# Spreading the residual gates' rows by DMA, and turning the modulation rows by transposes, in a two-layer fp32 encoder trunk

## What is computed

```
mod = (silu(c) @ w_mod[l] + b_mod[l])
sh1, sc1, g1, sh2, sc2, g2 = split(mod, 6)
h  = rmsnorm(x, norm1_g[l]) * (1 + sc1) + sh1
mixed = three branches of h (attention, convolution, state space), gated and summed
x  = x + g1 * (mixed @ w_out[l])
h2 = rmsnorm(x, norm2_g[l]) * (1 + sc2) + sh2
x  = x + g2 * ((silu(gate(h2)) * up(h2)) @ w_ffn_out[l])
```

## Time and profile before

| what | value |
|---|---|
| median of three runs | 1031.75 us |
| the profiled execution: its time | 1028.69 us |
| its span, first to last instruction | 1026.9 us |
| mean granted TensorE clock | 0.972 of full speed |
| PE busy | 946.5 us, 92% |
| DVE, ACT busy | 669.1 us, 464.6 us |
| DMA share of 16 engines (SP's queue) | 55.8%, 192.85 MB |

### The profile page before, as it was taken

How to read it: one execution, slowest core, us unless ns; L and a number is a source line. 1 busy time by engine, 2 the same in 40 slices (tenths; PEclk the granted TensorE clock), 3 DMA queues, 4 the chain that set the end, 5 groups by cost and what they waited for, 6 DMA issues and landing times.

```text
span 1026.9 us, 16212 instructions
## 1 busy us (share of the span) xinstructions
PE 946.5 (92%) x6911; PEld 795.2 (77%) x6911; DVE 669.1 (65%) x910; ACT 464.6 (45%) x544; POOL 8.7 (1%) x11
## 2 busy tenths in 40 slices
PE   5688998999998899999998999999999799999995
PEld 2487985666776878898996997666676599999994
DVE  3783878999575485456446576899966654444445
ACT  4484135623643465545335332564264453434342
POOL 2000000000000000000000000000000000000000
PEclk9798899999999999999999999999999999999998
DMA  9955235548666446465657534454867625555521
GB/s 340 234 201 206 83 125 204 204 135 292 256 253 156 164 167 244 166 228 204 223 166 162 165 104 175 174 211 158 273 230 280 212 92 179 191 186 184 192 96 41
DMA packets 128023, 194.01 MB, mean 189 GB/s; under 512 B 30706, under 2 KB 90618, under 8 KB 121808
## 3 DMA queue, kind: packets, MB, share of 16 engines
q1 hardware_dynamic: 127608, 192.85, 55.8%
q10 hardware_dynamic: 344, 0.14, 0.1%
HBM read 191.93 MB, written 1.05 MB: 188 GB/s over the span
## 4 chain that ended last, share of the span: by engine, by line
PE 65%; DVE 23%; ACT 4%; DMA 3%; issue 3%; SPq 0%; ACTq 0%; DVEq 0%
PE bank L537 18%; PE bank L538 17%; PE bank L539 17%; DVE wlo L1316 7%; DVE yc L1597 7%; PE bank L573 3%; DMA raw<-in_w_mod 2%; PE bank L629 2%; PE bank L602 2%; ACT whi L978 1%; PE bank L652 1%; DMA raw<-in_w_out 1%; PE bank L640 1%; DVE h L1490 1%; PE bank L728 1%
## 5 line engine op out<-in xcount | busy, mean ns | idle before, releaser
L1316 DVE TENSOR_TENSOR wlo<-raw,whi 128x2048 fp32r<-128x2048 f32 x132 | 302.1, 2290 | 237.5 <-PE bank L539 191.1
L978 ACT ACTIVATE whi<-raw 128x2048 fp32r<-128x2048 f32 x132 | 252.3, 1911 | 160.0 <-DMA raw<-in_w_in 73.0
L537 PE MATMUL bank<-hhi,whi 128*128 128x256 f32 x992 | 287.5, 290 | 7.1 <-DVE hlo L1495 4.0
L538 PE MATMUL bank<-hlo,whi 128*128 128x256 f32 x992 | 282.8, 285 | 0.0
L539 PE MATMUL bank<-hhi,wlo 128*128 128x256 f32 x992 | 282.7, 285 | 0.0
L537 PEld LDWEIGHTS bank<-hhi,whi 128*128 128x128 f32 x992 | 192.4, 194 | 16.3 <-issue 10.4
L538 PEld LDWEIGHTS bank<-hlo,whi 128*128 128x128 f32 x992 | 192.6, 194 | 0.6
L539 PEld LDWEIGHTS bank<-hhi,wlo 128*128 128x128 f32 x992 | 192.4, 194 | 0.0
L537 PE MATMUL bank<-whi,bhi 128*128 128x512 f32 x304 | 121.4, 399 | 3.4 <-DVE wlo L1316 3.4
L538 PE MATMUL bank<-wlo,bhi 128*128 128x512 f32 x304 | 119.1, 392 | 0.0
L539 PE MATMUL bank<-whi,blo 128*128 128x512 f32 x304 | 118.8, 391 | 0.0
(11 more groups left out here) (247 smaller groups left out, 839.4 us busy)
## 6 DMA issues: line engine op xcount, KB each, us to landing
raw<-in_w_mod SPq DMA_DIRECT2D x48, 1024.0 KB, 7.3
raw<-in_w_ffn_in SPq DMA_DIRECT2D x44, 1024.0 KB, 5.2
raw<-in_w_in SPq DMA_DIRECT2D x38, 1024.0 KB, 5.4
raw<-in_w_ffn_out SPq DMA_DIRECT2D x22, 1024.0 KB, 5.0
raw<-in_w_out SPq DMA_DIRECT2D x8, 1024.0 KB, 6.9
raw<-in_w_in SPq DMA_DIRECT2D x16, 256.0 KB, 5.1
raw<-in_ssm_glu_b SPq DMA_DIRECT2D x4, 1024.0 KB, 5.1
raw<-in_ssm_glu_a SPq DMA_DIRECT2D x4, 1024.0 KB, 5.1
```

Source lines behind the costliest of these rows:

```text
L537: mm(o, w_hi, a_hi, start=start, stop=False, skip_group_check=True)
L538: mm(o, w_hi, a_lo, start=False, stop=False, skip_group_check=True)
L978: fn(whi[mi % N_HI][:, :], raw[SLOT[item]][:, :], ACT.Copy).then_inc(s_hi, 1)
L1316: V.tensor_tensor(wlo[mi % N_LO][:, :], raw[SLOT[("main", *divmod(mi, NB))]][:, :], whi[mi % N_HI][:, :].bitcast(F32), ALU.subtract).then_ ...
```

## The change

`g_rows` on PE, `g_copy` on ACT, the list `G_AT` and the semaphore `g_tr` go. In their place SP issues, for each gate, two DMAs that read one row of `modrow` (one partition, 2 KB) 128 times and write it to 128 partitions. The places are in SP's list: `g1` before piece k = 4 of group 2 of its layer; `g2` of layer 0 before piece k = 4 of layer 1's group 0; `g2` of layer 1 behind the load of block `fo 0` (block 37). The bias load moves from piece k = 4 to k = 6, and its wait on `g_tr` becomes a wait for the landing of the spread. `mod_columns` makes four 128x128 transposes, and `mod_vectors` reads every 32nd column of their result.

```diff
+        def spread_gate(eng, l, ng):
+            eng.wait_ge(mod_row, 3 * l + ng + 1)
+            eng.wait_ge(s_ready, 2 * l + 2)
+            eng.wait_ge(ys_lo, l + 1)
+            for half in range(2):
+                r = 32 * (2 * (ng - 1) + half)
+                dst = (g1 if ng == 1 else g2)[:, half * 512:(half + 1) * 512]
+                eng.dma_start(dst, modrow[r:r + 1, :].rearrange("p (o n) -> p o n", o=1).to_broadcast([1, P, 512])).then_inc(g_ready, 16)
...
                     _, l, ng, k = item
-                    if k == 4 and (l, ng) != (0, 0):
+                    if k == 4 and ng == 2:
+                        spread_gate(sp, l, 1)
+                    if k == 4 and l and ng == 0:
+                        spread_gate(sp, l - 1, 2)
+                    if k == 6 and (l, ng) != (0, 0):
                         sp.wait_ge(mod_tr, 3 * l + ng)
                         if ng != 1:
-                            sp.wait_ge(g_tr, 4 * l + (2 if ng == 2 else 0))
+                            sp.wait_ge(g_ready, 16 * (4 * l + (2 if ng == 2 else 0)))
                         load_bias(sp, l, ng)
...
+                    if item[1:] == (DEPTH - 1, AT[("fo", 0)]):
+                        spread_gate(sp, DEPTH - 1, 2)
                     if item[1:] == (DEPTH - 1, AT[("fg", 0)]):
                         sp.wait_ge(s_ready, 2 * DEPTH)
...
                 for j in range(4):
-                    last = mm(b_mod[:, 4 * j:4 * j + 4], modrow[:, j * P:(j + 1) * P], consts[:, 0:4], start=(j == 0), stop=(j == 3), skip_group_check=True)
+                    last = nc.tensor.transpose(b_mod[:, j * P:(j + 1) * P], modrow[:, j * P:(j + 1) * P], ident[:, :])
                 last.then_inc(mod_tr, 1)
-
-            def g_rows(l, ng, half):
-                pe.wait_ge(mod_row, 3 * l + ng + 1)
...
-                mm(b_y[:, :], ones[r:r + 1, :], modrow[r:r + 1, :], start=True, stop=True, skip_group_check=True).then_inc(g_tr, 1)
...
-            def g_copy(l, ng, half):
...
-                fn(dst[:, half * 512:(half + 1) * 512], b_y[:, :], ACT.Copy).then_inc(g_ready, 1)
...
-                V.tensor_copy(modv[:, c0:c0 + 16].rearrange("p (q j) -> p j q", q=4), b_mod[:, 0:16].rearrange("p (j q) -> p j q", q=4)).then_inc(mod_ready, 1)
+                V.tensor_copy(modv[:, c0:c0 + 16].rearrange("p (q j) -> p j q", q=4), b_mod[:, :].rearrange("p (j r) -> p j r", j=4)[:, :, 0:P:32]).then_inc(mod_ready, 1)
```

More of the change, by code:

```diff
@@ L160 @@
 MIX_TURN_AT = {2 * AT[("cp", 1)] + 1: (0, 1), 2 * AT[("wo", 0)]: (2,), 2 * AT[("wo", 0)] + 1: (3,)}
-G_AT = {2 * (i + 2 + half) + 1: (m[0], half) for i, m in MOD_AT[0].items() if m[1] == DK - 1 for half in range(2)}
 PREP_AT = AT[("fg", 1)]
@@ L371, in trunk @@
             sem(n) for n in "ldt_spread vec_tr vec_cp c_tr silu_c c_ready".split())
-        row_zero, s_bias, mod_row, mod_tr, mod_ready, scale_ready, g_tr, g_ready = (
-            sem(n) for n in "row_zero bias_landed mod_row mod_tr mod_ready scale_ready g_tr g_ready".split())
+        row_zero, s_bias, mod_row, mod_tr, mod_ready, scale_ready, g_ready = (
+            sem(n) for n in "row_zero bias_landed mod_row mod_tr mod_ready scale_ready g_ready".split())
         sq_ready, rb_ready, rms_ready, diag_ready, xt_ready, h_full, hhi_ready, hlo_ready = (
@@ L846, in small_columns @@
                 if l:
-                    pe.wait_ge(g_ready, 4 * l)
+                    pe.wait_ge(v_ready, l)
                 nc.tensor.transpose(b_y[:, 0:VROWS], rows, ident[0:VROWS, 0:VROWS])
@@ L892, in side @@
                     mix_turn(l, g)
-                if t in G_AT:
-                    g_rows(l, *G_AT[t])
                 if t in (CONV_MEAN_AT, CONV_VAR_AT):
@@ L1209, in side @@
                     mix_hi(l, g)
-                if t in G_AT:
-                    g_copy(l, *G_AT[t])
                 if l == 0 and t in ROUND_AT[0]:
@@ L1658, in post @@
                         if t == 0 and u == 0:
-                            dve.wait_ge(g_ready, 4 * l + 2)
+                            dve.wait_ge(g_ready, 16 * (4 * l + 2))
                         tt(flat(tmp), bank[BANK_OF[(l, i - 1, t)]][:, :], g1[:, cols], ALU.mult).then_inc(wo_read, 1)
@@ L1674, in post @@
                 elif kind == "fo" and n == NF - 1:
-                    dve.wait_ge(g_ready, 4 * l + 4)
+                    dve.wait_ge(g_ready, 16 * (4 * l + 4))
                     for t in range(TILES):
```

## The result

The changed kernel takes 1064.88 us (median of 4 runs, 1060.56 to 1066.43); the kernel before, beside it, 1031.76 us (1031.64 to 1034.16). The ratio is 1.0309, with a 95% interval from 1.0273 to 1.0344: slower. The profiled execution is 1066.0 us with a span of 1064.2 us, 37.3 us above the profiled execution of before (1028.69 and 1026.9). The mean granted clock is 0.948 of full speed against 0.972, and among the four executions the time follows it (1066.43 at 0.949, 1063.75 at 0.953, 1060.56 at 0.958).

What follows compares the result with a forecast made beforehand. PE was taken as the bound (65% of the chain, DVE 23%). Lateness of 28.8 + 8.6 minus 6.15 removed gave 31.3 us: 1060.0 profiled, 1063 us median with 3.1 added; own range 1050 to 1074, with the fast rival 1024 to 1072.

Steps and rivals of the forecast that it cites:

- R: Time to spread both halves of one gate from one source partition each: 18.6 us, 9.3 us a half; forecast's chance 0.60.
- the load over 64 partitions: Attention weights' load in the profile before: 226 GB/s against 396 over 128 partitions; divided by eight places, 28.3 GB/s each.
- The loads behind them: Loads after a spread in SP's queue wait for it: block 25's lands at 767.4 us, block 46's at 422.4.
- The rival of the full rate: Spreads run at nearly full rate, R up to 4: all loads in time, 6.15 us gained, 1025.6 us; chance 0.27.
- The bound below R: Lower bound from the store of 256 KB from 128 partitions: some 1.5 us engine time for two at 396 GB/s.
- Twice the room: Rival: reads have twice the room, R = 9.3; `g1` costs 2 x 5.1, sum +4.1, 1035.8 us; chance 0.08.
- `g1`: 14.4 us forecast: In each layer, block 25's load comes late behind the spread, PE begins block 26 14.4 us late; both layers 28.8 us.
- `g2` of layer 0: 8.6 us forecast: Block 46's load comes late behind the spread, so DVE's `lo` starts at 424.3 instead of 415.66: 8.6 us.
- `g2` of layer 1: nothing, as forecast: Behind block 37's load the spread ends at 834.8, block 38's load at 837.4, read at 845.64: hidden, no cost.
- What is removed: Work taken from PE and ACT: row products for `g2` 4.2 us, column sets 1.05 and 0.9; together 6.15 us gained.
- The first set: First set of column products on PE's chain, 1.85 us, halved by transposes: 0.9 us gained.
- the third: One of three column sets on PE's chain, 0.79 us by products against 0.44 by transposes: 0.35 us gained.

Runs made afterwards that it cites:

- the half-size spreads: The changed kernel with each spread moving 256 of its 512 numbers, in as many packets: 1034.77 us, ratio 1.0033 against the kernel before.
- the kernel without spreads: The changed kernel without any spread or the waits for it, gates holding other contents: 1025.7 us, ratio 0.9946 against the kernel before.
- neither part alone: The kernel before with only columns by transposes: 1032.74 us; with only row products, copies and their waits gone and the bias load moved: 1029.46 us.
- the kernel with 128 sources: The changed kernel with each spread reading 128 partitions of modrow one to one, same bytes: 1024.12 us, ratio 0.9936 against the kernel before.
- The transposes alone: The kernel before with only the columns made by transposes, row products kept: 1032.74 us, ratio 1.0015 against the kernel before.

## Why the prediction held, point by point

**The price of the spread.** The term that decides all was R, forecast as 18.6 us for a gate from the load over 64 partitions: 28.3 GB/s for one place in SBUF. The windows show 26 to 29 GB/s for some 14 us, and a mixed edge at either end; the two halves of a gate land 9.0 us apart, where 9.3 were forecast. The loads behind them land as forecast. In layer 1 the load of block 25 landed at 773.77 + 19.29 = 793.06; the forecast was 767.4 on the clock of before, and SP's issue ahead of the spread had moved from 738.49 to 765.03, by 26.5 us: 793.9. For block 46 it was 422.4, plus 12.2 us of lateness: 434.6; ACT took it up at 434.27. The rival of the full rate fell; what spoke for it, that the row was of writes, counts for nothing, as reads have the same limit. (The bound below R, "some 1.5 us" for two halves at 396 GB/s, should be 1.3; nothing rests on it.) Twice the room (R = 9.3) fell as well, and the half-size spreads show that its number would have been right had the rate been so: expected +4.1 us against before, measured 3.1.

**`g1`: 14.4 us forecast, 12.9 and 12.7 measured.** The path was as told. In layer 1 the load landed 0.8 us before its forecast, and PE began block 26 at 807.63, which is 807.63 - 767.45 - 26.5 = 13.7 us late; a further 0.9 us is made up by the next milestone.

**`g2` of layer 0: 8.6 us forecast, 11.4 measured.** This is the step that failed in size, "so DVE's `lo` of block 46 starts at 424.3 instead of 415.66". I took ACT's copy as the one thing that `lo` waits for. The timeline of the kernel after, ACT, DVE and PE:

```profile
431.69 1.91 ACT L980 ACTIVATE whi<-raw 128x2048 fp32r<-128x2048 f32 x1 [12.36 <-DMA raw<-in_w_ffn_in]
433.51 0.58 ACT L1030 ACTIVATE blx<-bank 128x512 f32<-128x512 f32 x1
434.27 1.91 ACT L980 ACTIVATE whi<-raw 128x2048 fp32r<-128x2048 f32 x1 [0.18 <-DMA raw<-in_w_ffn_out]
...
439.27 2.29 DVE L1308 TENSOR_TENSOR wlo<-raw,whi 128x2048 fp32r<-128x2048 f32 x1 [3.34 <-PE bank L553]
...
424.22 0.28 PE L553 MATMUL bank<-hhi,wlo 128*128 128x256 f32 x1
434.23 1.09 PE L754 MATMUL bank<-ident,ca 128*128 128x128 f32 x4 [9.73 <-ACT blx L1030]
434.97 0.56 PE L551 MATMUL bank<-hhi,whi 128*128 128x256 f32 x1
435.33 0.42 PE L552 MATMUL bank<-hlo,whi 128*128 128x256 f32 x1
```

`lo` of block 46 starts at 439.27 and not at 424.3 + 12.2 = 436.5, and what it waits for is PE. PE had stopped in the middle of block 44 for 9.73 us, at four transposes that prepare layer 1. They wait for ACT's copy `blx`, a small one, which stands in ACT's order behind the copy of block 45 and so behind its load. It is a second way from the load to PE, one block earlier than the one I followed, and I did not look for it: of the load of block 45 I asked only when it frees the next, and not what else stands behind its reader. A stopped PE also comes back slowly, as the last two lines show: 0.56 and 0.42 us for what took 0.28. The granted clock of that stretch:

```profile
430.00:434.00 4.00, 0.00 (x0) 0.00 (x0) 0.37 (x1) 2.31 (x2) 0.00 (x0) 0.50 1.05 378
434.00:438.00 4.00, 3.77 (x20) 3.80 (x21) 1.93 (x1) 2.48 (x3) 0.00 (x0) 0.57 0.27 88
438.00:442.00 4.00, 4.00 (x34) 3.03 (x33) 2.73 (x2) 0.60 (x1) 0.00 (x0) 1.00 0.13 29
```

It is at the lower of its two levels (1.2 of 2.4 GHz, 0.50) when PE resumes, and back at 1.00 by 438 us. A wait of PE costs more than its length.

**`g2` of layer 1: nothing, as forecast.** From the milestone at 787.0 to the end the kernel after gains 2.0 us, where the two row products and the set of columns there promised 2.45.

**What is removed.** Between the milestones at 284.7 and 321.4 two row products and a set of columns give 2.7 us, against 2.45 forecast; at the end they give 2.0. The first set (0.9 forecast) and the third (0.35) show as 0.1 each. That is 4.9 us of 6.15 in this execution; the kernel without spreads has 6.2 by the medians, but neither part alone shows its share. That 6.2 met 6.15 so well is partly luck: between the two profiled executions the kernel without spreads gains 4.4 us (spans of 1026.9 and 1022.5), and that of before was a fast one.

**The sum.** In the profiled execution the three spreads make 37.0 us and the removed work -4.9, together 32.1 against the 31.3 forecast. The other 5.2 us lie in stretches without any work of the change. One is 2.1 us between 321 and 390, where the granted clock is 0.90 instead of 0.95; the kernel with 128 sources takes much the same there (70.2 us at 0.90, against 70.5), so the slow spreads aren't the cause. The other is 3.1 us between 634.6 and 653.1, where the kernel after has this row for the work that took 18.50 us at a clock of 1.00 before:

```profile
658.10:679.70 21.60, 18.12 (x74) 13.33 (x73) 14.98 (x27) 10.61 (x16) 0.00 (x0) 0.84 0.39 146
```

The transposes alone have a dip in the same stretch, and the kernel without spreads takes 21.6 us there at 0.84, so it isn't the spreads' doing. So behind the forecast of 1063 us and the median of 1064.88 stand errors that partly cancel: 3.2 us too much for the two `g1`, 2.8 too little for `g2` of layer 0, 1.2 too much gain, and 5.2 us of lower clock that no term stood for.

The last step, from the profiled execution to the median, came near by luck. The prediction added 3.1 us, the distance for the kernel before. For the kernel after the median lies 1.1 us below the profiled execution (1064.88 and 1066.0). So the profiled execution was missed by 6.0 us (1060.0 forecast), and the median by 1.9 only because the 3.1 us filled half of the gap.

## What to carry to other kernels

A row that all partitions need can come by DMA, but the source has to lie in many partitions: a broadcast from one partition moves some 28 GB/s and meanwhile holds all 16 engines. A transfer from another queue gets only a packet in between on each of them. Keep the row in 32 partitions, which costs only a wider bias load where the matmul and the addition that make the row have that size anyway, and spread it 32 to 32. When a load is made late, follow everything that stands behind its reader in that engine's order, small copies too, and not only the reader's own result.

## What the runs showed of the hardware that was not expected

- **A DMA's issue can hold the issuing engine.** SP's issue of a 1 MB load mostly takes 0.37 to 0.6 us (in the kernel before the longest is 3.7), but 6.8 and 9.6 us behind the spreads (246.53 and 253.35 above), and 9.31 where the spreads were issued by POOL. I had taken the issue as free. The profile gives no reason; the Trainium skill's page "Perfetto Trace Analysis", section "DMA Instruction — HWDGE (DVE, Sync)", counts in the reported time of such an instruction a wait for the descriptor generator's lock and the generating, which would fit a generator that can't hand on its descriptors. No run here isolates it.
- **Partitions 0 and 32 together give 25 GB/s, 0 and 64 give 41**, read at the same time by two queues. A 2 KB packet from partition 0 takes 1.08 us in the first case and 0.08 in the second.
- **A small gain can be given back.** The same 74 or 75 matmuls and 27 DVE operations took 18.5, 20.6 and 21.6 us in three kernels at granted clocks of 1.00, 0.92 and 0.84, in a stretch that holds no edited work. Whether the transposes elsewhere bring this about is open.
